# Hybrid attention layer: group B's values eighteen pairs behind its scores, loads ordered across head groups, query reordering shared with GpSimd

## The reference, cut to what matters

```python
B_CONFIGS = ((128, 1), (512, 4), (2048, 16))

def reference(x, mem, pre_norm, w_in, sink_a, mem_norm, w_mem_kv, w_out, post_norm):
    ...
        u = rms_norm(h, pre_norm[l])
        proj = jnp.einsum('bsd,de->bse', u, w_in[l])
        qa, ka, va, ga, qb, kb, vb, gb, qc, gc = jnp.split(proj, IN_SPLITS, axis=-1)
        ...
        oa, _ = banded_attention(qa * scale, ka, va, A_WINDOW - 1, sink)
        ...
        for (win, dil) in B_CONFIGS:
            qs = to_strided(qb * scale, dil)[:, :, :, None, :]
            o, lse = banded_attention(qs, to_strided(kb, dil), to_strided(vb, dil),
                                      win // dil, None)
            ...
        wts = jax.nn.softmax(jnp.stack(lses, axis=0), axis=0)
        ob = jnp.sum(wts[..., None] * jnp.stack(outs, axis=0), axis=0)
        ...
        pc = jax.nn.softmax(sc, axis=-1)
        oc = jnp.einsum('bhsm,bmhd->bshd', pc, mv.astype(jnp.float32))
        ...
        y = jnp.concatenate([oa * jax.nn.silu(ga), ob * jax.nn.silu(gb),
                             oc * jax.nn.silu(gc)], axis=-1)
        y = jnp.einsum('bse,ed->bsd', y, w_out[l])
        h = h + rms_norm(y, post_norm[l])
```

## Time and profile before

| | us |
|---|---|
| median of 3 runs | 2551.96 |
| lowest, highest | 2549.57, 2558.19 |
| the profiled execution | 2556.23 |
| its span, first to last instruction | 2554.3 |
| PE, DVE, ACT, POOL busy in it | 2284.1, 1311.7, 1182.8, 88.2 |
| mean granted clock of PE | 0.942 |
| projection stage | 0 to 1182.2 |
| rounds B0 to B11, with the first slots of A0 | 1191.0 to 1763.8 |
| from A's first scores to C's first scores | 1763.8 to 2033.1 |
| from C's first scores to the last value product | 2033.1 to about 2182 |
| finish stage, from its first product | 2196.5 to 2554.3 |

### The profile page before, as it was taken

How to read it: one execution, slowest core, us unless ns; L and a number is a source line. 1 busy time by engine, 2 the same in 40 slices (tenths; PEclk the granted TensorE clock), 3 DMA queues, 4 the chain that set the end, 5 groups by cost and what they waited for, 6 DMA issues and landing times.

```text
span 2554.3 us, 43511 instructions
## 1 busy us (share of the span) xinstructions
PE 2284.1 (89%) x13644; PEld 1914.6 (75%) x13644; DVE 1311.7 (51%) x3975; ACT 1182.8 (46%) x3055; POOL 88.2 (3%) x103
## 2 busy tenths in 40 slices
PE   5999999999999999998788898887868678799998
PEld 5887788878887788877677687776757567688887
DVE  4751257223751357102577777676768567333333
ACT  4223532244223521214788787775657567322221
POOL 0000000000000000010000000000111101000000
PEclk9999999999999999998799898888879789899999
DMA  5346334553455334474637737647467655444443
GB/s 186 132 170 169 121 125 141 172 152 111 141 180 156 128 111 148 143 206 98 116 79 137 149 68 147 129 78 143 105 139 153 141 139 124 158 148 147 140 140 115
DMA packets 349581, 350.36 MB, mean 137 GB/s; under 512 B 151440, under 2 KB 278032, under 8 KB 345360
## 3 DMA queue, kind: packets, MB, share of 16 engines
q1 hardware_dynamic: 341872, 322.78, 46.9%
q0 software_dynamic: 7584, 26.22, 4.2%
HBM read 222.32 MB, written 126.62 MB: 137 GB/s over the span
## 4 chain that ended last, share of the span: by engine, by line
PE 32%; DVE 6%; issue 5%; ACT 5%; DMA 3%; SPq 1%; POOL 1%; DVEq 0%; POOLq 0%; ACTq 0%
PE a_ps_o L984 6%; PE f_ps L58 5%; PE f_ps L59 5%; PE f_ps L60 5%; PE a_ps_t L1000 4%; PE a_ps_s L937 4%; ACT probs L1174 3%; PE a_ps_s L938 3%; DVE probs L1031 2%; DVE probs L1118 1%; DMA scratch_y<-a_gate 1%; DVE probs L1147 1%; DMA k_lo<-scratch_qk_lo 1%; ACT a_pT L1198 1%; PE a_ps_s L955 1%
## 5 line engine op out<-in xcount | busy, mean ns | idle before, releaser
L58 PE MATMUL p_ps<-p_uT_hi,p_w_hi 128*128 128x512 f32 x1536 | 603.1, 393 | 3.5 <-DVE p_w_lo L389 3.5
L59 PE MATMUL p_ps<-p_uT_lo,p_w_hi 128*128 128x512 f32 x1536 | 598.8, 390 | 0.0
L60 PE MATMUL p_ps<-p_uT_hi,p_w_lo 128*128 128x512 f32 x1536 | 598.7, 390 | 0.0
L1174 ACT ACTIVATE probs<-probs,a_stat 128x256 f32<-128x256 f32 (+1 forms) x896 | 433.3, 489 | 63.5 <-DVE a_stat L1031 61.9
L1031 DVE CUSTOM_DVE_ANT_0 probs<-a_ps_s,a_maskB 128x256 f32<-128x256 f32 (+1 forms) x704 | 251.2, 395 | 215.1 <-PE a_ps_s L938 207.0
L58 PEld LDWEIGHTS p_ps<-p_uT_hi,p_w_hi 128*128 128x128 f32 x1536 | 289.3, 188 | 63.6 <-issue 4.0
L60 PEld LDWEIGHTS p_ps<-p_uT_hi,p_w_lo 128*128 128x128 f32 x1536 | 288.9, 188 | 60.5
L59 PEld LDWEIGHTS p_ps<-p_uT_lo,p_w_hi 128*128 128x128 f32 x1536 | 289.2, 188 | 58.9
L937 PE MATMUL a_ps_s<-k_hi,q 128*128 128x256 f32 (+1 forms) x768 | 259.1, 354 | 72.4 <-POOL q L609 27.7
L1198 ACT ACTIVATE a_pT<-a_ps_t 128x512 f32<-128x512 f32 (+1 forms) x412 | 230.2, 562 | 197.8 <-PE a_ps_t L1000 196.8
L389 DVE TENSOR_TENSOR p_w_lo<-p_w_raw,p_w_hi 128x1024 fp32r<-128x1024 f32 x96 | 117.6, 1225 | 393.3 <-ACT p_w_hi L286 374.8
(11 more groups left out here) (120 smaller groups left out, 2446.6 us busy)
## 6 DMA issues: line engine op xcount, KB each, us to landing
p_w_raw<-in_w_in SPq DMA_DIRECT2D x96, 512.0 KB, 4.0
scratch_qk_hi<-p_o_hi SPq DMA_DIRECT2D x96, 256.0 KB, 2.0
scratch_qk_lo<-p_o_lo SPq DMA_DIRECT2D x96, 256.0 KB, 2.4
a_v<-scratch_v SPq DMA_DIRECT2D x40, 512.0 KB, 7.4
p_x<-in_x SPq DMA_DIRECT2D x32, 512.0 KB, 4.2
scratch_v<-p_o_v SPq DMA_DIRECT2D x256, 64.0 KB, 2.0
scratch_gate<-p_rot SPq DMA_DIRECT2D x64, 256.0 KB, 2.2
a_gate<-scratch_gate SPq DMA_DIRECT2D x64, 256.0 KB, 4.2
```

Of the source, the lines that this page charges most:

```text
L58: nc.tensor.matmul(out, w_hi, m_hi, start=first, stop=False)
L59: nc.tensor.matmul(out, w_hi, m_lo, start=False, stop=False)
L60: return nc.tensor.matmul(out, w_lo, m_hi, start=False, stop=last)
L1174: last = nc.scalar.activation(place, place, ACT.Exp, scale=-1.0, bias=stat[:, s, 0, u.column:u.column + 1], accum_out=stat[:, s, 1, u.colu ...
```

## The change

**Distance.** B's TAIL is 18. The exchange's steps stand at slots 1 (DVE), 4 (PE), 5 and 6 (DVE), 7 (ACT), 9 and 10 (DVE), 13 (PE), 14 (DVE); scaling with the new coefficients begins at slot 15. A0 keeps 24 slots, A1 has 22, and A's scores begin at slot 11. The four far additions are split, two a slot (`finish_rest`), and the gate multiplies a slot later.

**Queries of B.** ACT makes the four pieces of place 1 in slots 1, 3, 5 and 7. POOL makes the natural order in one instruction per phase, as soon as the phase before is scored; PE waits for it at slot 12 (`natural_copied`).

**Loads.** SP's list is written out over the groups. A's second key head goes to a place of its own (`later_keys`, in the room of the probabilities that A doesn't use) during A's phases 2 and 3. C's keys and values for all four heads are loaded once, ahead of A's gate for phase 5. C's first queries stand ahead of A's last gate. Each head's queries in A are asked for two phases ahead.

**POOL's list.** In A the copy of phase n+3 stands ahead of the store of phase n. The eight output weights follow A's first eight stores.

**Constants** lie in one block (`fixed`) and are loaded by POOL in the projection stage, when the third quarter is done. **Loops:** A and C are written out in PE's, DVE's and ACT's programs; B keeps its loop.

The diff, cut to its core:

```diff
@@ project_stage, POOL
+                pool.wait_ge(multiplied, 3 * NT * NCH)
+                pool.dma_start(early.consts.ident, io["ident"]).then_inc(early.consts_loaded, 16)
...
@@ head_group
-    Q_SLOTS = {1: 0, 2: 1, 3: 2, 4: 3, 6: 4, 7: 5, 9: 6, 10: 7}
-    Q_ORDER = {8: 1, 9: 2, 10: 3, 11: 4, 12: 6, 20: 8}
+    Q_SLOTS = {1: 0, 3: 1, 5: 2, 7: 3}
+    Q_ORDER = {8: 1, 9: 2, 10: 3, 11: 4}
...
-    COPIES = {"B": 8, "A": 1, "C": 0}[kind]
+    COPIES = {"B": 4, "A": 1, "C": 0}[kind]
...
-    TAIL = 12 if kind == "B" else 4
+    TAIL = 18 if kind == "B" else 4
@@ load_k
+                (hi_place, lo_place), row, done = later_keys, KA + HD, k_loaded[1][s]
+                sp.wait_ge(prev.turned, prev.TOTAL - 8)
@@ loads, all memory keys at once
+        def load_memory(first):
+            sp.wait_ge(first.values_done, first.TOTAL)
+            sp.dma_start(buf.masks["B4"], io["maskC"]).then_inc(mask_loaded, 16)
+            for part, place in ((sc["mk_hi"], k_hi), (sc["mk_lo"], k_lo)):
+                for half in range(2):
+                    dst = place[half * HD:(half + 1) * HD, :].rearrange("p (h n) -> p h n", n=NMEM)
+                    sp.dma_start(dst.bitcast(F32), part.rearrange("(h p) n -> p h n", p=HD)).then_inc(k_loaded[0][0], 16)
...
@@ tensor_parts
+            if kind == "B" and slot == 12:
+                ge(pe, natural_copied, number(phase))
...
-            if kind == "B" and slot == 2:
+            if kind == "B" and slot == 4:
                 pe.wait_ge(spread, p + 1)
...
-            if kind == "B" and slot == 6:
+            if kind == "B" and slot == 13:
                 pe.wait_ge(spread_back, p + 1)
@@ vector_parts
+        def finish_rest(phase, d):
+            if kind == "B" and last_of.get(d, -1) >= MERGED:
+                c = last_of[d] - MERGED
+                add_far(c, 1).then_inc(bank_read, 1)
@@ copy_queries on POOL
+        if kind == "B":
+            pool.wait_ge(scores_ready, p * NP)
+            pool.wait_ge(q_loaded, 32 * p)
+            natural_queries(nc, q, 2, natural_copied)
             return
@@ SP's list
+                B, A, C = (g.loads(sp) for g in groups)
+                for h in range(6):
+                    B.k(h, 1)
+                    if h == 0:
+                        B.v(0, 0)
+                    B.q(h, 1)
+                    B.gate(h, 0)
+                    if h > 0:
+                        B.v(h, 0)
+                    if h < 5:
+                        B.q(h + 1, 0)
+                        B.k(h + 1, 0)
+                    else:
+                        A.q(0, 0)
+                        A.k(0, 0)
+                        A.mask()
+                    B.v(h, 1)
+                    B.gate(h, 1)
...
+                for m in range(2, 12):
+                    h, s = m // 2, m % 2
+                    if m < 10:
+                        A.q(h + 1, s)
+                    if m < 4:
+                        A.k(3, s)
+                    if m == 5:
+                        C.memory(groups[0])
+                    if h == 3:
+                        A.v(3, s)
+                    if m == 11:
+                        C.q(0, 0)
+                    A.gate(h, s)
+                for m in range(8):
+                    if m < 7:
+                        C.q((m + 1) // 2, (m + 1) % 2)
+                    C.gate(m // 2, m % 2)
@@ POOL's list
+                for m in range(1, 12):
+                    B.copy_queries(pool, m // 2, m % 2)
+                    if m > 1:
+                        B.store(pool, m // 2 - 1, m % 2)
...
+                for m in range(12):
+                    if m + 3 < 12:
+                        A.copy_queries(pool, (m + 3) // 2, (m + 3) % 2)
+                    A.store(pool, m // 2, m % 2)
+                    if m < KD:
+                        load_w(m)
```

262 lines of the change are left out of this document (125 added, 137 removed).

## The result

The changed kernel takes 2427.8 us (median of four runs, 2418.2 to 2432.9) where the kernel before takes 2551.9: ratio 0.9506, 95% interval 0.9472 to 0.954. It is 124 us faster; 186 had been predicted. The profiled execution took 2427.5 us with a span of 2425.6, 128.7 us shorter than before's.

A forecast was written before the change was run, and what follows sets the result against it. No engine was full: TensorE waited on exchange, copies and loads, each wait followed by a low clock, with ScalarE and TensorE next. Terms -60 -9 -20 -59 -30 -5 -3 = -186 gave 2370, adjusted to 2366 us; range 2335 to 2405.

The forecast's parts named there:

- Term 3: Filling and draining of B: B1 shorter by 9 us, the drain from B to A by 20 us.
- Term 5: Group C: memory keys loaded once during A, rounds of 13.0 us, seven rounds 30 us shorter.
- Term 6: The ends: constants loaded earlier, start 5 us sooner; output weights moved into A, end of C 3 us shorter.
- Term 1: Group B's full rounds: exchange and key waits go, 428 us instead of 488, 60 us less.
- I take 43: Length in us chosen for a full round of B, between a lower bound of 36.7 and an upper of 46.
- rival (c): B runs at ACT's 40.5 us in all rounds with casts hidden, 25 us less: 2341 us; chance 0.12.
- Term 2: POOL's cast in B: each holds DVE for 1.45 us, 0 to 16 us for 11 casts, inside the 43.
- Term 4: Group A: copies and loads come earlier, DVE binds, ten rounds at 14.6 us, 59 us less.
- rival (a): B stays, the exchange's wait turning into small ACT and DVE waits; B gives 15 instead of 60: 2411 us; chance 0.09.
- the 11.4 us stretch: Eight slots of B from 1325.7 us with ACT busy 10.9; used for B's lower bound and against rival (a).
- Rival (d): Straight code for A and C costs 4.2 us in each of 14 rounds, +59: 2425 us; chance 0.05.
- Rival (b): Casts hold DVE in the open, transfers hold A and C, +32: 2398 us; chance 0.12.

The follow-up runs named there:

- cast_later: Against fill: GpSimd's cast of B's queries waits until score slot 5 of its round is done instead of starting with the round; 2366.2 us.
- all_out: Against the changed kernel: B's loop written out as straight code on TensorE, VectorE and ScalarE; 2404.1 us.
- shift68: Against the changed kernel: 68 already met wait instructions added on TensorE ahead of the attention, so B's loop starts 68 instructions later; 2428.0 us.
- pe_out: Against the changed kernel: B's loop written out on TensorE only, VectorE's and ScalarE's loops kept; 2422.8 us.
- fill: Against all_out: six products of constants, read by nobody, added on TensorE at the start of B's rounds 4, 6, 8 and 10; 2391.4 us.
- later_weights: Against cast_later: the output weights loaded in C's first four rounds instead of behind A's stores; 2361.7 us.
- fill_a_act: Against fill: from A's fourth phase, ScalarE lays out the natural order of A's queries in four pieces instead of GpSimd's cast; 2413.2 us.
- before_ac_out: Against the kernel before: the loops over the heads of A and C written out, B's loop kept; 2547.9 us.
- fill_all: Against fill: B's second values and gates loaded at the next even round's start, B's stores issued by SyncE, output weights loaded in C's rounds; 2376.7 us.

## Why the prediction missed, point by point

**Direction and most terms held.** Term 3 (B1 -9.8, drain -18), Term 5 (-31.5, 12.9 us a round) and Term 6's start (-5.8) came within 3 us. PE's wait at the second exchange product is gone, as are the waits for A's second keys and C's first queries.

**Term 1 failed by 34 us**, in its step "I take 43". As sums of busy time the working was good: with the clock kept, an even and an odd round take 37.8 and 42.4 us (cast_later, the loops written out), 40.1 on average. That is rival (c)'s 40.5, less than the forecast. For the eight rounds B3 to B10 the step gives 344 us, and 382.3 were measured. The runs split the gap. The loop's turns cost 29.0 (all_out's 353.3). From there to cast_later's 321.0 it is another 32.3: 25 in the even rounds, which run at the low clock in part, and 7 in the odd ones at full clock, by the casts' place. For what is left, 43 a round was 23 too long. Besides the turns the step left out that PE's pace is no constant. It treated the clock as something that rises when the long waits go ("if PE's pace counted in half of them"). The runs show a fall at pauses that stay: about 4 us and more at the loop's turn in the changed kernel, 1 to 2 us with the loop written out. From then on PE itself is the bound: busy 45.0 of 45.6 us at 0.81 in all_out's B4. The ten big waits of the earlier trace rows were gone, and what was left was enough: the clock in B's full rounds is 0.90 after as before.

**The loop's turn.** Of the loop in B the prediction says "this loop stays". Its turn was charged as 4.20 us of DVE in an even round and thought to be covered. all_out prices the turns at 24 us in the whole kernel (29 in B3 to B10 of the profiled runs). PE's own fetching, which no row of before showed, goes with the code's place and cost 0 to 5 us of the medians (shift68, pe_out).

**Term 2 failed in its place, not in its price.** 1.45 us of hold is near what a cast alone cost (2.25 for two scales that take 0.5 to 0.6). But the text put the casts "at the start of a round", with the store of two phases before behind them. The store falls due at slot 21, POOL's list is in order, and the next cast starts as soon as the store is issued, twice around each odd round, and the hold is 3 us. The hold itself is the smaller damage, 7 us of the eight rounds. It makes PE pause near a turn, and the clock does the rest: 25 us in all between fill and cast_later. The Trainium skill (SBUF — State Buffer, section Who interferes with whom), on which the prediction drew, speaks of a hold for one whole instruction. The trace agrees for the cast alone (1.98 us beside a cast of 1.90); with two issues ahead the hold began in the second issue, so there it was longer than the cast (2.96 us).

**Term 4 failed by 19 us.** "The loads have more than ten us to spare there" was wrong at one place: the four loads of the second head's keys stood ahead of a gate load in SyncE's list, while the output weights ran in the same rounds, and DVE waited 6.98 us for the gate. The step had reckoned with a DMA share of 0.8; A3 to A6 ran at 1.02 to 1.17. A5 took 23.6 us, partly at the low clock. That is 9 of the 19 us. The rest was not taken apart by a run; the trace shows casts that fall on scales, and short falls of the clock in every second round or so (0.89 and 0.90 in A3, A7, A9). A took 15.6 us a round at best, in later_weights. Whether 14.6 can be had without the casts on POOL was not shown: fill_a_act put another wait in their place.

**Term 6's end (-3 became +2).** The weights' loads were indeed gone, and DVE waited 3.28 us for PE's last values instead. The gap ahead of the finish is 17.3 instead of 15.1 us. No run was made for this.

**The range.** The case that came true is rival (a): the exchange's wait turned into small waits, and B gave 26 us where (a) said 15. It got 0.09 and was left out of the range, "Against: the 11.4 us stretch", eight slots at the clock of 0.96. With (a), B's 11 us more, and A and the end as they were measured, the sum is 2411 - 11 + 19 + 5 = 2424. Rival (d) has nearly the measured number, 2425, by a mechanism that before_ac_out and all_out exclude. Rival (b) had both of the causes that were found in A and at the casts, and priced them by their length alone. Neither it nor the range up to 2405 had a price for the clock's falls or for ACT's turn of the loop.

## What to carry to other kernels

Before costing a removed wait, ask what the clock does with the pauses that are left: where PE is the next bound, a pause of 1 to 2 us at the same spot in every second round cost some 7 us each here, and single repairs measured as nothing until all pauses of the spot were closed. When edits that plainly do their work (the waits are gone in the trace) leave the time unchanged, compare the granted clock round by round; here four of them in a row moved nothing, and products of constants in the pause with one number in a wait gave 38 us. Where an engine's list is in order, work out when each entry comes due relative to its neighbours: the cast was costed right and stood in the wrong place.

## What the runs showed of the hardware

- In B's rounds the granted clock fell to its lower level at the same places in kernel after kernel: during or just behind pauses of 0.5 to 2.4 us at the turn from an odd to an even round (up to 5.5 us with the loop kept), or of 0.8 to 1.2 us behind a cast's hold. It rose again 3 to 27 us later. Not every such pause did it: 0.64 and 0.99 us ahead of all_out's B10 did not, and 0.65 and 1.19 us brought it down in two of fill_all's four even rounds. With the turn's pause filled by products of constants and the cast five slots later (cast_later) it stayed up from B1 to B10.
- Two DMA issues on GpSimd followed by a cast held a DVE scale for 3.0 us, from inside the issues to the cast's end; the cast alone 1.2 to 2.1; the issues alone did not hold one visibly (0.54 us for two scales beside a store's issue in cast_later).
- A loop of TensorE can be fetched anew at each turn in one place (nine packets of some 16 KB a turn) and stay resident 68 instructions further on. ScalarE stood still at its own turns in either: four times, 13.5 us in all and up to 4.3, in shift68, three times and 9.8 us in the changed kernel.
- In the loops' kernels PE's refetching (some 7 us a turn) and ScalarE's turn lay over each other; taking one away showed the other in full.
